# Hybrid attention and Fourier encoder layer on eight cores: the head of each sequence reordered, conversions spaced, Fourier weights applied last

## What is computed

```python
h = rmsnorm(x, g_mix)
q, k, v, f = split(h @ w_in)                 # 1024, 1024, 1024, 512 columns
q, k = rope(rmsnorm(q, g_q)), rope(rmsnorm(k, g_k))      # 16 maps of 64
a = softmax(q k^T / 8)                       # 2 maps for each of 8 heads
o = rmsnorm((a[2h] - lam * a[2h+1]) @ v, g_sub) * 0.8
attn_out = o @ w_attn_br
fr = real(fft2(f))                           # over tokens and over 128 channels of a group
four_out = fr @ w_four_br
gates = sigmoid(h @ w_gate + b_gate)
x = x + (gates0 * attn_out + gates1 * four_out) @ w_out
h2 = rmsnorm(x, g_mlp)
y = x + square(relu(h2 @ w_up)) @ w_down
```

## Time and profile before

| | us |
|---|---|
| three runs: median | 4910.66 |
| lowest, highest | 4700.29, 5039.23 |
| the profiled execution | 4703.16 |
| its span, slowest core (core 4) | 4701.6 |
| spans of the eight cores | 4682.7 to 4701.6 |
| PE busy | 4242.8 (90%) |
| DVE, ACT, POOL busy | 57%, 56%, 11% |

### The profile page before, as it was taken

The page is one execution under the profiler, slowest core; times in us unless marked ns, Lnnn a source line. Parts: engine busy times, 40 slices in busy tenths (PEclk is TensorE's granted clock), DMA queues, the critical chain, the costliest instruction groups (busy, mean ns, idle before and its releaser), DMA issues.

```text
span 4701.6 us, 56711 instructions; the slowest of 8 cores (4682.7 to 4701.6 us)
## 1 busy us (share of the span) xinstructions
PE 4242.8 (90%) x22188; PEld 1650.2 (35%) x22188; DVE 2662.3 (57%) x4140; ACT 2639.9 (56%) x3542; POOL 531.9 (11%) x565
## 2 busy tenths in 40 slices
PE   4787779999999887999999999988899999999998
PEld 1332123333333433333333333343333333333333
DVE  1465647475574465755647556446674655746552
ACT  2357846566564465655656566446565665656620
POOL 0264000000000054000000000015300000000000
PEclk9898889999999999999999999999999999999999
DMA  9567973533434513334353343542334334343343
GB/s 179 142 115 137 145 156 115 178 124 118 174 116 169 178 73 122 117 124 169 108 191 117 126 167 106 187 149 78 127 130 156 134 130 159 130 166 123 125 158 124
DMA packets 186139, 651.10 MB, mean 138 GB/s; under 512 B 14096, under 2 KB 88976, under 8 KB 144400
## 3 DMA queue, kind: packets, MB, share of 16 engines
q1 hardware_dynamic: 128448, 563.58, 35.3%
q0 software_dynamic: 57424, 83.89, 9.9%
HBM read 599.19 MB, written 115.34 MB: 152 GB/s over the span
## 4 chain that ended last, share of the span: by engine, by line
PE 72%; ACT 10%; DVE 8%; DMA 5%; POOL 2%; issue 1%; another core or an unknown queue 0%; SPq 0%; ACTq 0%; DVEq 0%; POOLq 0%
PE pall L257 68%; ACT sb_ov L272 9%; DVE sb_ov L275 7%; PE pall L259 4%; POOL sb_ov L275 2%; DMA wb_vf<-w_in 1%; DMA sb_ov<-fr_s 1%; DMA sb_ov<-x 1%; DVE sb_ov L281 1%; DMA sb_ov<-wb_qk 1%; DMA sb_ov<-wb_g 1%; DVE sb_ov L290 1%; DVE sb_ov L278 0%; ACT sb_sm L272 0%
## 5 line engine op out<-in xcount | busy, mean ns | idle before, releaser
L257 PE MATMUL pall<-sb_ov 128*128 128x512 bf16 (+2 forms) x17280 | 3766.0, 385 | 302.2 <-ACT sb_ov L272 103.2
L272 ACT ACTIVATE sb_ov<-pall 128x1024 bf16<-128x1024 f32 (+2 forms) x2268 | 1938.1, 901 | 1438.4 <-PE pall L257 1356.2
L257 PEld LDWEIGHTS pall<-sb_ov 128*128 128x128 bf16 (+1 forms) x17280 | 1429.2, 98 | 2385.1 <-issue 493.1
L275 DVE TENSOR_TENSOR sb_ov<-sb_ov 128x1024 bf16<-128x1024 bf16 (+4 forms) x2316 | 1407.7, 631 | 382.9 <-ACT sb_ov L272 301.7
L275 POOL TENSOR_TENSOR sb_ov<-sb_ov 128x512 f32<-128x512 bf16 (+1 forms) x492 | 470.4, 971 | 3889.4 <-PE pall L257 2247.3
L275 DVE TENSOR_TENSOR sb_ov<-pall,sb_ov 128x512 f32<-128x512 f32 (+3 forms) x744 | 522.9, 708 | 474.6 <-PE pall L257 452.8
L272 ACT ACTIVATE sb_ov<-sb_ov 128x512 f32<-128x512 f32 (+1 forms) x480 | 340.8, 712 | 118.5 <-DVE sb_ov L275 44.2
L257 PE MATMUL pall<-sb_ov,sb_cmat 128*128 128x512 bf16 x1008 | 291.9, 391 | 83.5 <-DVE sb_ov L290 55.3
L259 PE MATMUL pall<-sb_ov,sb_cmat 128*32 128x512 bf16 x3072 | 314.2, 399 | 0.1
L281 DVE TENSOR_SCALAR sb_ov<-sb_ov,sb_sm 128x1024 bf16<-128x1024 f32 x192 | 144.5, 753 | 283.8 <-ACT sb_sm L272 180.8
L272 ACT ACTIVATE sb_ov<-pall,sb_vecs 128x512 f32<-128x512 f32 x192 | 130.6, 687 | 212.6 <-PE pall L257 212.4
(11 more groups left out here) (33 smaller groups left out, 274.9 us busy)
## 6 DMA issues: line engine op xcount, KB each, us to landing
sb_ov<-wb_up SPq DMA_DIRECT2D x96, 1024.0 KB, 4.9
sb_ov<-wb_down SPq DMA_DIRECT2D x96, 1024.0 KB, 6.2
sb_ov<-k_s SPq DMA_DIRECT2D x96, 512.0 KB, 5.0
sb_ov<-wb_g SPq DMA_DIRECT2D x48, 1024.0 KB, 11.3
sb_ov<-v_s SPq DMA_DIRECT2D x96, 512.0 KB, 6.4
sb_ov<-wb_af SPq DMA_DIRECT2D x48, 768.0 KB, 7.9
sb_ov<-x SPq DMA_DIRECT2D x48, 512.0 KB, 5.1
sb_ov<-x POOLq DMA_DIRECT2D x12, 2048.0 KB, 11.9
```

Source lines behind the costliest of these rows:

```text
L257: P.op("pe", lambda e: e.matmul(out, lhsT=lhsT, rhs=rhs, start=start, stop=stop), reads, writes)
L272: P.op("act", lambda e: e.activation(out=out, in_=in_, func=func, **kw), reads, writes)
L275: P.op(eng, lambda e: e.tensor_tensor(out=out, in0=in0, in1=in1, op=op), reads, writes)
```

## The change

1. **Head of s = 0.** The three `vf` blocks are no longer converted by DMA first. Their float32 halves (1 MB each) are loaded by SP into the unused `O_UT` region (`w_first`) and cast into the ring slots by DVE and ACT (`w_conv`). x loads come ahead and between. Tiles 0 to 3 run block by block. The conversion of `vf` for s = 1, 2 goes to the end of `late_list`.
2. **Head of s = 1, 2.** x tiles 0 and 1 are loaded at slot 143 of the last attention chunk before and normalized at slots 159 and 162, between the gate tiles, in other addresses (`x_at`, `hb_at`). The loads of the cos, sin and Fourier tables move from the start of the head to t = 5.
3. **Last tiles, all s.** Tiles 12 to 15 are projected together after tile 15's transpose, block by block, so that each `vf` slot is released after its four tiles and the loads of `dft` and `qk` can start.
4. **Conversions spaced.** The eight `qk` conversions (`conv_qk`), all at the start before, are issued after tile 3 and tile 9 (two each) and at tau = 0, 8, 16, 24 of the rope stage of s = 0 (one each). Each names a cell among its reads: a `P_HT` tile, or the first cell of `P_PREP`, which is also the first cell of the buffer that stB of even n writes. The late ones are popped at tau % 6 == 3 (every 4th tau before) and every 11th slot of attention (every 3rd before).
5. **Rope stage.** The cos multiply on POOL moves from stG to stE, and stG(tau-2) comes ahead of stE(tau-1). `o_rs` has 4 buffers (3 before), `o_xn` 2 (3 before). The Fourier generator yields 3 for 2 before its closing matmuls, and 2 between its two groups of DVE writes; the credit is 2.6 for 2.4 (156 credits of steps for 140).
6. **Fill.** All 8 attention tiles first, then x1, then the 8 Fourier tiles. The weights are two `at` blocks and one `fo` block of 1 MB for four `af` blocks of 0.75 MB.
7. **Kind c.** Each selection matmul uses only the 64 rows that are not zero, in an order that alternates the two row halves.
8. **CELL** is 256 for 512.

```diff
-CELL = 512
+CELL = 256
-        for c, c0 in ((0, 2048), (2, 3072), (1, 2560)):
-            conv(wb_vf[c].rearrange("p (k n) -> p k n", k=8), w_in_r[:, :, c0:c0 + 512], ("wvf", c))
-        for hp in range(4):
+        def conv_qk(n, after):
+            hp, w = n // 2, n % 2
             d = wb_qk[hp].rearrange("p (w k n) -> p w k n", w=2, k=8)
...
+            DMA("pool", d[:, w], w_in_r[:, :, w * 1024 + hp * 256:w * 1024 + (hp + 1) * 256], ("cvq", n), after, [("wqk", hp, w)])
...
             for j in range(8):
-                if j % 2 == 0:
-                    wlo, wr = wuse((s, qc, "af", j // 2))
-                if j == 2:
-                    DMA("pool", ovf(O_X1, 8192).rearrange("p (t d) -> p t d", t=4), x_d[r0:r0 + 512, :].rearrange("(t p) d -> p t d", p=128),
-                        "x1", [], ovc(O_X1, 8192))
+                if j % 4 == 0:
+                    wlo, wr = wuse((s, qc, "at", j // 4))
...
                 TT(ovf(o_s0, 1024), bank(bA), ovf(o_s0, 1024), ALU.mult, [bres(bA)] + ovc(o_s0, 1024), ovc(o_s0, 1024))
...
+            DMA("pool", ovf(O_X1, 8192).rearrange("p (t d) -> p t d", t=4), x_d[r0:r0 + 512, :].rearrange("(t p) d -> p t d", p=128),
+                "x1", [], ovc(O_X1, 8192))
+            wlo, wr = wuse((s, qc, "fo"))
+            for j in range(8):
                 bB = fb()
                 for g in range(4):
...
                 TT(ovf(o_s1, 1024), bank(bB), ovf(o_s1, 1024), ALU.mult, [bres(bB)] + ovc(o_s1, 1024), ovc(o_s1, 1024))
                 TT(ovb(O_MIX + j * 512, 512), ovf(o_s0, 1024), ovf(o_s1, 1024), ALU.add, ovc(o_s0, 2048), ovc(O_MIX + j * 512, 512))
...
             elif kind == "c":
-                for m, sel in ((0, sel1), (1, sel2)):
-                    MM(bank(2 * sl + m), sel, ovb(O_LH, 512), True, False, ovc(O_LH, 512) + ["cmat"], [bres(2 * sl + m)])
-                    MM(bank(2 * sl + m), sel, ovb(O_LH + 512, 512), False, True, ovc(O_LH + 512, 512) + ["cmat"], [bres(2 * sl + m)])
+                for part in range(2):
+                    for m, sel in ((0, sel1), (1, sel2)):
+                        rows = slice(64 * m, 64 * m + 64)
+                        MM(bank(2 * sl + m), sel[rows, :], ov[rows, O_LH + part * 512:O_LH + part * 512 + 512], part == 0, part == 1,
+                           ovc(O_LH + part * 512, 512) + ["cmat"], [bres(2 * sl + m)])
...
+            elif s + 1 < nseq:
+                at(base + 143, lambda: (x_load(s + 1, 0), x_load(s + 1, 1)))
+                at(base + 159, lambda: a0_norm(s + 1, 0))
+                at(base + 162, lambda: a0_norm(s + 1, 1))
...
-                    if late_list and i % 3 == 0:
+                    if late_list and i % 11 == 0:
                         late_list.pop(0)()
...
+            def w_first(i, c0):
+                for hf in range(2):
+                    l2 = O_UT + (i % 2) * 8192 + hf * 4096
+                    DMA("sp", ovf(l2, 4096).rearrange("p (k n) -> p k n", k=4), w_in_r[:, 4 * hf:4 * hf + 4, c0:c0 + 512], ("wf", i % 2, hf), [], ovc(l2, 4096))
+
+            def w_conv(i):
+                for hf in range(2):
+                    l2 = O_UT + (i % 2) * 8192 + hf * 4096
+                    r2 = O_RING + i * 4096 + hf * 2048
+                    CP(ovb(r2, 2048), ovf(l2, 4096), ovc(l2, 4096), [("ringh", i, hf)], eng="act" if hf else "dve")
+
+            if s == 0:
+                x_load(s, 0)
+                w_first(0, 2048)
+                x_load(s, 1)
+                w_first(1, 3072)
+                x_load(s, 2)
+                a0_norm(s, 0)
+                a0_norm(s, 1)
+                x_load(s, 3)
+                x_load(s, 4)
+            else:
+                for t in (2, 3, 4):
+                    x_load(s, t)
             a0_tr(0)
...
+            if s == 0:
+                w_conv(0)
+                w_first(2, 2560)
...
+            for t in range(NT):
+                if t + 2 < NT:
+                    a0_norm(s, t + 2)
+                    if t + 5 < NT:
+                        x_load(s, t + 5)
+                if t + 1 < NT:
+                    a0_tr(t + 1)
+                if s == 0 and t < 4:
+                    if t == 1:
+                        proj(0, 0)
+                        proj(1, 0)
+                    if t == 2:
+                        w_conv(1)
+                    if t == 3:
+                        proj(2, 0)
+                        proj(3, 0)
+                        w_conv(2)
+                        for c in (2, 1):
+                            for t4 in range(4):
+                                proj(t4, c)
+                elif t < 12:
+                    proj(t, 0)
+                    proj(t, 2)
+                    proj(t, 1)
+                elif t == 15:
+                    for c in (0, 2, 1):
+                        for t4 in range(12, 16):
+                            proj(t4, c)
                         wdone((s, "vf", c))
+                        cur[0] += LAG
+                        wpump()
+                vdone(t)
+                if t == 5:
+                    DMA("sp", ovb(P_TB, 4096), dft_d[0], "tb", [], ovc(P_TB, 4096))
+                    rope_load()
+                if s == 0 and t in (3, 9):
+                    for n in ((0, 1) if t == 3 else (2, 3)):
+                        conv_qk(n, ovc(P_HT + t * 1024, 1024))
...
-                        yield 2
+                        yield 3
...
                             TT(frT[:, g, 1:2048:4], bank(6), ws, ALU.add, rd, wrc)
+                            yield 2
                             TT(frT[:, g, 2047:0:-4], bank(6), ws, ALU.subtract, rd, wrc)
...
-                        yield 3
+                        yield 2
...
+                o_t1 = o_t1_[n % 2]
+                ca, cr = cosT(n % 4)
+                TT(ovf(o_t1, 1024), ovb(o_xn, 512), ca, ALU.mult, ovc(o_xn, 512) + cr, ovc(o_t1, 1024), eng="pool")
...
-                dcr += 2.4
+                dcr += 2.6
...
+                if 0 <= tau - 2 < NU:
+                    stG(tau - 2)
                 if 0 <= tau - 1 < NU:
                     stE(tau - 1)
-                if 0 <= tau - 2 < NU:
-                    stG(tau - 2)
...
-                if late_list and tau % 4 == 0:
+                if s == 0 and tau % 8 == 0 and tau < 32:
+                    conv_qk(4 + tau // 8, ovc(P_PREP, 256))
+                elif s == 0 and late_list and tau % 6 == 3:
                     late_list.pop(0)()
```

More of the change, by code:

```diff
@@ L381, in wchunk_fill @@
         def wchunk_fill(s, qc):
-            for jp in range(4):
-                wadd((s, qc, "af", jp), wb_af[jp], 3072, [("waf", jp, 0), ("waf", jp, 1)], "sp")
+            for ch in range(2):
+                wadd((s, qc, "at", ch), wb_at[ch], 4096, [("wat", ch)], "sp")
+            wadd((s, qc, "fo"), wb_fo, 4096, [("wfo",)], "sp")
             for ch in range(2):
@@ L407, in wissue @@
             src, ncols, reads, q, view = wlist[i]
+            if i < 3:
+                return
             while any(r not in P.writer for r in reads):
@@ L421, in wpump @@
                     break
-                if any(r not in P.writer for r in wlist[i][2]):
+                if i >= 3 and any(r not in P.writer for r in wlist[i][2]):
                     break
@@ L750, in attention @@
                     if i == GATE_AT:
-                        assert fill[0] is None and not late_list
+                        assert fill[0] is None
                     gate_tile(s, qc, i - GATE_AT)
@@ L926, in prep @@
             o_sq_ = [PB + 512 * i for i in range(2)]
-            o_rs_ = [PB + 1024 + 1024 * i for i in range(3)]
-            o_xn_ = [PB + 4096 + 512 * i for i in range(3)]
-            o_t1_ = [PB + 5632 + 1024 * i for i in range(2)]
+            o_rs_ = [PB + 1024 + 1024 * i for i in range(4)]
+            o_xn_ = [PB + 5120 + 512 * i for i in range(2)]
+            o_t1_ = [PB + 6144 + 1024 * i for i in range(2)]
             NU = 64
```

94 lines of the change are left out of this document (43 added, 51 removed).

## The result

| | before, us | after, us |
|---|---|---|
| the profiled execution | 4703.16 | 4577.99 |
| its span, slowest core | 4701.6 | 4576.4 |
| spans of the eight cores | 4682.7 to 4701.6 | 4539.5 to 4576.4 |
| lowest run | 4700.29 | 4571.52 |
| median of four runs | 4806.30 | 4748.76 |

The kernel after takes 0.9731 of the time before, with a 95% interval of 0.9689 to 0.9773: 2.7% faster.

A forecast was written before the change was run, and what follows sets the result against it. PE was taken to bound the kernel (72% of the chain that ended last, DMA 5%), with idle time at five kinds of place. The terms sum to -184 us: 4703 - 184 = 4519, range 4455 to 4595.

The forecast's parts named there:

- x1's place in the queue of chunk (0,1): Chunk (0,1): x1 queues behind two conversions instead of many, its later place costs nothing: -10 us (0, -11).
- the cause of the wait for DVE's PSUM writes in the rope stages: Rope stages: one DVE write a tau instead of two leaves stE in time, removing most of 10.4 us of waits.
- the seams: Heads of s = 1, 2: PE starts after 2.5 us for 13; -12 us each, -24 in all (-14, -27).
- the bubble: Last tiles of a head: batching tiles 12 to 15 leaves PE 3.6 us idle before the last transpose.
- the price of kind c with the Fourier tiles: Kind c: -26 us (0, -40) over 96 heads; eight Fourier tiles in a row: +11 us (0, +30) in 11 chunks.
- the loss in the rope of s = 0: Rope of s = 0: four conversions make stB wait, +33 us against -18 gained; +15 in all (-10, +45).
- The first head: Head of s = 0: first rope matmul at 130 us for 193.5, -63 us (-45, -75).
- The Fourier result: First chunk with a fill, each sequence: the wait for the Fourier result goes three times, -33 us (-28, -37).
- Rivals 2 and 4: First head stays bound by DMA, 4544 us, chance 0.10; stB waits long on conversions, 4819 us, chance 0.04.
- The sign listed under "wrong": Sign against the forecast: a chunk (0,1) that waits for up or down conversions, issued as late as its slot 33.
- rival 1: Rope stage does not get shorter because DVE, not the order, holds it: 4573 us, chance 0.15.
- rival 3: Draining the array on the tiling change eats kind c's gain: 4545 us, chance 0.08.

## Why the prediction was right in sign and 55 us too high in gain

Four steps failed, by 15 to 23 us each: x1's place in the queue of chunk (0,1), the cause of the wait for DVE's PSUM writes in the rope stages, the seams with the bubble, and the price of kind c with the Fourier tiles. One term, the loss in the rope of s = 0, was 11 too high and hides part of them.

**Right.** *The first head*: -63 and -62.8, first rope matmul at 132.8 for 130, first projection at 29.95 for 27. That it fits so closely is in part luck: of 9 us of waits for the third block and x5 2.7 came, while the bubble (2.72 and 2.53 idle), the slower matmuls behind it (96 in 22.76) and at the start (16 in 5.64) took about 9 where I had 4. *The Fourier result*: the wait of the earlier trace rows is gone; chunks (1,0) and (2,0) lost 13.8 to 14.0 with their waits and clock, 11 predicted for the wait. *Chunk (0,0)*'s full DMA engines cost PE nothing there, as said. Rivals 2 and 4 (a first head bound by DMA, conversions that take 85 us) did not come: the conversions landed in 7 to 10 us in the rope stage. The sign listed under "wrong" that came is the last one: chunk (0,1) waits behind the up and down conversions.

**Chunk (0,1): 23 us of the missing 55.** The step "in (0,1) it is behind two conversions instead of many: -10 (0, -11)" failed. On the profiled core it was five, in full DMA engines, 65 us from issue to landing; over the eight cores three to five, and four to six before. "Its later place costs nothing" holds for the issue (7.6 us ahead of the chunk, 9.1 before), but the landing stayed where it was (38 to 60 us into the chunk, 39 to 62 before) while the reader came earlier: the 12 us won in the same chunk by the Fourier result went into the wait for x1 (8.99 before, 14.17 now). Loading x1 early gave 14.6 back. My bound for this term had no loss in it; I had no row for a landing in that queue of after, and should have counted the conversions by their rate. Every 11th slot of the plan is no distance in time either: POOL issued 17 conversions from 350 to 545 us, one each 11.5 us on the mean and four of them within 2.2 us, and they landed some 14 us apart.

**Rope of s = 1, 2: 19 us.** "Most of the 13.3 goes" was right. "One DVE write a tau instead of two leaves stE in time: most of the 10.4" failed: L276 kept 10.9. I took that wait for DVE's queue; it was PE's next write to bank 6. The bank swap removed it and gave the 9 to 11 us. So rival 1 (DVE's load holds the stage) was not the cause either.

**Heads of s = 1, 2: 15 us.** The seam gave about 8 of the 12: the 2.5 us for transpose and multiply are right as lengths, and ACT had caught up by the last sigmoid, as I had it. What the sum left out is that the multiply stands behind a scaling on DVE which needs ACT's table load and two activations after that sigmoid. As for the rule that I had set beside it (the Trainium skill, ScalarE: Activation LUTs, What ACT_TABLE_LOAD costs), the trace of after shows 1.28 us a load with the next activation 0.02 us behind its end (1443.01, 1444.31): no drain beyond the row appears here, and the shortfall has another cause. The bubble was 5 to 6 us instead of 3.6, because I left out the clock that follows it.

**Kind c and the Fourier tiles.** The term of -26 was too large: about 6 us in ten filled chunks and 5.3 in chunk (0,0), where I had counted none. The saving of matmul time is there (a head's four take 0.66 us for 0.96, 5.3 us for 8 heads; I had 0.55 for 1.03), but three quarters of it do not shorten the chunk: ACT sets the next matmul for the mean, the gap before it grows, and the granted clock falls behind the longer gap. Against the wait for x1 in chunk (0,1) even the rest was lost, so that the time is rival 3's (no gain from kind c) without its mechanism. The tiling rule (the Trainium skill, TensorEngine Tiling (Array Packing), Key Properties) isn't needed for that: the busy time fell. The Fourier tiles cost 1.4 us a chunk for the 1 predicted. Together the two are why the steady chunks rose by 0.1 to 1.6 us where -1.4 was forecast.

**Rope of s = 0: 11 us better.** With all qk conversions out of it the stage took 186.0, which is 18.8 less than before: the 18 of gain were there. That they match is luck, since s = 1 and 2 won only 8.5; this stage began 10.7 us longer than theirs, and what held it before was not taken apart. The four conversions cost 22.4, not 33: 16.0 by the named cell, for ACT waited 5.2 us each time instead of 8 and never the 6 more, and 6.4 without it. The two make the +3.6 measured. The tail's +1.7 is within the scatter.

Added up from the table: 23 (chunk (0,1)) + 19 (ropes of s = 1, 2) + 15 (their heads) + 16 (steady filled chunks) + 2 (tail) - 11 (rope of s = 0) - 5 (chunk (0,0)) - 3 (c10 and c20) = 56; the 55 but for the rounding of the terms.

## What to carry to other kernels

Ask of every wait that goes what the same reader waits for next, and whether that one is set by a queue that no engine's speed moves: here a DMA behind a backlog of conversions kept its landing time, so each us won between its issue and its reader was lost at it. A wait named after an engine (PE for DVE) can be its load, its order, or a buffer used again; a bank swap or a reordering of one instruction tells them apart cheaply. And count the slower clock after a pause with the pause, after short ones too: a saving that only lengthens a gap can cost more than it gives.

## What was not expected of the hardware

- A load queued behind casting DMAs while the DMA engines were full took 53.8, 64.9 and 71.4 us for 2 MB on the profiled cores of three kernels, 11.7 us at the median elsewhere; the conversions landed some 14 us apart for each MB of output. Which cores waited for it differed: the same chunk took 292 us on one and 313 on another.
- The granted clock fell to 0.5, the lower of its two levels (1.2 of 2.4 GHz), behind pauses of very different length: 24 matmuls took 7.03 us after 3.96 us idle and 5.34 after 0.89. It also fell, for 3.4 us, behind three gaps of 0.41, 0.24 and 1.12 us in a row, and not behind 0.42, 0.26 and 0.69.
- Selection matmuls of 64 rows on alternating halves save PE time (0.3 us for a group of four), and yet 0.6 us a chunk is what is left where PE is the bound.
